# A decoder block on eight Trainium2 cores: a new order of loads and norms in its first stage, with unread matmuls on TensorE

## The reference, cut to what matters

```python
u = rms_norm(h, norm_mix[l])
proj = u @ w_in[l]                       # q | k | v (3 dilation groups x 8 heads x 64) | pool | gates
q = partial_rope(q, pos); k = partial_rope(k, pos)
att = dilated_attention(q, k, v)         # 3 groups: (window, dilation) = (128,1), (512,4), (2048,16)
...                                      # pooling mixer, gates, w_out, SwiGLU, final norm
```

## Time and profile before

| | us |
|---|---|
| median of 3 runs (lowest, highest) | 1216.14 (1214.82, 1222.4) |
| the profiled execution | 1215.8 |
| its span on the slowest core (core 5); all cores | 1214.3; 1207.6 to 1214.3 |
| TensorE busy in the span | 1155.9 (95%) |

### The profile page before, as it was taken

How to read it: one execution, slowest core, us unless ns; L and a number is a source line. 1 busy time by engine, 2 the same in 40 slices (tenths; PEclk the granted TensorE clock), 3 DMA queues, 4 the chain that set the end, 5 groups by cost and what they waited for, 6 DMA issues and landing times.

```text
span 1214.3 us, 21698 instructions; the slowest of 8 cores (1207.6 to 1214.3 us)
## 1 busy us (share of the span) xinstructions
PE 1155.9 (95%) x8470; PEld 644.7 (53%) x8470; DVE 575.4 (47%) x883; ACT 443.9 (37%) x728; POOL 68.9 (6%) x134
## 2 busy tenths in 40 slices
PE   3888899999999999799999999999999999999997
PEld 2454766586676666344444444444444444444477
DVE  3346566755654558875333467422213233122455
ACT  3464545745655564563222133311120032111213
POOL 0001000000001110100111100000000000000000
PEclk9899999999999999999999999999999999999999
DMA  8837633233323331212555523244612813446733
GB/s 201 235 113 207 138 80 75 48 76 80 76 50 81 76 58 40 53 22 39 136 146 111 76 46 52 53 74 88 115 28 52 148 35 70 78 80 112 154 116 106
DMA packets 33764, 109.98 MB, mean 91 GB/s; under 512 B 4736, under 2 KB 12160, under 8 KB 27776
## 3 DMA queue, kind: packets, MB, share of 16 engines
q0 software_dynamic: 15264, 69.76, 30.8%
q1 hardware_dynamic: 18400, 38.84, 11.0%
HBM read 148.31 MB, written 16.06 MB: 135 GB/s over the span
## 4 chain that ended last, share of the span: by engine, by line
PE 87%; DVE 5%; DMA 3%; ACT 2%; issue 2%; SPq 0%; DVEq 0%; POOL 0%; ACTq 0%; POOLq 0%
PE ps_p L197 50%; PE ps_s L197 18%; PE ps_o L197 16%; PE ps_o L200 3%; DMA wp<-w_in 1%; DVE uto L210 1%; DMA rin<-qk 1%; DVE ta L207 1%; DVE rt L207 1%; ACT rs L204 1%; DMA qk<-rout 1%; DVE acc L207 1%; DMA rout<-rp 0%; DVE uth L210 0%; DVE ftv L210 0%
## 5 line engine op out<-in xcount | busy, mean ns | idle before, releaser
L197 PE MATMUL ps_p<-uto,wp 128*128 128x512 bf16 (+1 forms) x784 | 182.7, 386 | 15.7 <-DVE uto L210 6.9
L197 PE MATMUL ps_s<-ftv,wguv 128*128 128x512 bf16 x640 | 144.7, 379 | 0.0
L197 PE MATMUL ps_o<-ftv,wguv 128*128 128x512 bf16 x640 | 144.7, 379 | 0.0
L197 PEld LDWEIGHTS ps_p<-uto,wp 128*128 128x128 bf16 x784 | 76.2, 100 | 108.2 <-issue 27.9
L197 PE MATMUL ps_p<-actt,wdv 128*128 128x512 bf16 (+2 forms) x704 | 115.7, 326 | 0.0
L204 ACT ACTIVATE qk<-ps_p 128x512 bf16<-128x512 f32 (+2 forms) x122 | 69.8, 577 | 108.4 <-PE ps_p L197 95.0
L207 DVE TENSOR_TENSOR acc<-ps_o,acc 128x1024 f32<-128x1024 f32 x32 | 64.9, 2030 | 84.6 <-PE ps_s L197 51.1
L197 PEld LDWEIGHTS ps_s<-ftv,wguv 128*128 128x128 bf16 x640 | 62.6, 98 | 75.5
L197 PEld LDWEIGHTS ps_o<-ftv,wguv 128*128 128x128 bf16 x640 | 62.6, 98 | 75.6
L197 PEld LDWEIGHTS ps_p<-wp,uto 128*128 128x128 bf16 x1536 | 95.0, 122 | 6.5 <-issue 1.8
L197 PE MATMUL ps_p<-wp,uto 128*128 128x128 bf16 x1536 | 97.7, 225 | 0.8 <-ACT qk L204 0.8
(11 more groups left out here) (120 smaller groups left out, 1433.3 us busy)
## 6 DMA issues: line engine op xcount, KB each, us to landing
wguv<-wgu POOLq DMA_DIRECT2D x20, 1024.0 KB, 7.7
wp<-w_in POOLq DMA_DIRECT2D x12, 768.0 KB, 7.4
wdv<-wd POOLq DMA_DIRECT2D x6, 1408.0 KB, 19.3
ht<-x SPq DMA_DIRECT2D x32, 256.0 KB, 5.0
xs<-x SPq DMA_DIRECT2D x3, 2048.0 KB, 17.6
xs<-x POOLq DMA_DIRECT2D x3, 2048.0 KB, 10.4
xs<-x SPq DMA_DIRECT2D x4, 1024.0 KB, 17.7
oT<-ost SPq DMA_DIRECT2D x12, 256.0 KB, 2.9
```

The lines of the kernel that those rows point to most:

```text
L197: return P.op("pe", lambda e: e.matmul(out, lhsT=lhsT, rhs=rhs, start=start, stop=stop), after)
```

## The change

- Loads: the second half of piece 0 is issued only when the first has landed, and pieces 2 to 7 each when the piece before has landed. The weights of unit 1 wait for the second half of piece 0, where they waited for half of piece 1. The masks wait for piece 3. Pieces 6 and 7 change buffers. The weights of unit 3 wait for the gather of unit 1.
- Squares: both halves' squares are issued ahead of the first items; some of the squares of pieces 1 and 2 go from ScalarE to VectorE; those of pieces 6 and 7 are cut in two and lie between other items.
- Items: unit 1 on piece 0 comes ahead of unit 0 on piece 1. Unit 0's v copies on own tokens go to ScalarE after piece 0.
- Attention: the first unit's steps start 13 items after its gather, the others' 15 as before.
- Ahead of everything a Ln of one column on ScalarE and 80 matmuls of 128x128 (the matrix of 1/1024 times itself) into `ps_o`, which nobody reads; 26 more of them after the sums of each half.

```diff
     def load_piece(i):
         if i == 0:
-            return [P.dma("sp", piece0[h], tile_of(x, 2048 * h, 8, 256), d_xh[0][h]) for h in range(2)]
+            t = P.dma("sp", piece0[0], tile_of(x, 0, 8, 256), d_xh[0][0])
+            return [t, P.dma("sp", piece0[1], tile_of(x, 2048, 8, 256), d_xh[0][1], after=[t])]
...
-        after = [t_u[(0, 1, 2, 4, 3)[i - 3]]] if i > 2 else [t_ld[1][1]]
+        after = [t_ld[i - 1][1]] + ([t_u[i - 3]] if i > 2 else [])
         if i == 7:
             after = after + [t_in0[0]]
...
+            ts.append(tt(o, p, p, ALU.mult, after=[t_ld[i][c // 4]]) if (i == 1 and c in (1, 3)) or (i == 2 and c % 2) else
+                      act(o, p, AF.Square, after=[t_ld[i][c // 4]]))
...
+    def idle_mm(n):
+
+        for _ in range(n):
+            mm(ps_o[:, 0:128], onev, onev, True, True, after=[t_one])
+
+    def half_piece(h, ts):
...
         t = act(r, r, AF.Exp, after=[bank_free[k]], scale=-0.5)
+        idle_mm(26)
         for c in range(8):
...
-            if u < 2:
+            if u < 2 and not on_act:
                 t_v[u] = bank_free[k] = P.op("dve", lambda e: e.tensor_copy(out=outv, in_=inv), [t, slot_free[g]])
...
-            ready[v] = n_item[0] + LAG
+            ready[v] = n_item[0] + (LAG if v else 13)
...
-    t_wp.append(P.dma("pool", wpv[1], tile_of(w_in, 3072, 8, 384), d_wp[1], after=[t_ld[1][0]]))
+    t_wp.append(P.dma("pool", wpv[1], tile_of(w_in, 3072, 8, 384), d_wp[1], after=[t_ld[0][1]]))
     t_ld += [load_piece(2)]
-    t_msk = P.dma("pool", mskv, msk, P.dsem())
...
-    half_piece(0)
+    act(rsv[1][:, 0:1], onev[:, 0:1], AF.Ln, after=[t_one])
+    idle_mm(80)
+    half_piece(0, half_squares(0))
+    ts = half_squares(1)
     for item in half_items(0):
         run(item)
-    half_piece(1)
+    half_piece(1, ts)
...
-    normalize(1, sq[1])
-    t_ld.append(load_piece(3))
-    for item in of(0, 1):
-        run(item)
-    sq.append(squares(2))
-    load_wp(2, [t_ld[2][1]])
-    for k, item in enumerate(of(1, 0) + of(1, 1)):
+    for k, item in enumerate(of(1, 0) + of(0, 1) + of(1, 1)):
         run(item)
         if k == 1:
+            normalize(1, sq[1])
+            t_ld.append(load_piece(3))
+            load_wp(2, [t_ld[2][1]])
+            t_msk = P.dma("pool", mskv, msk, P.dsem(), after=[t_ld[3][1]])
+        if k == 3:
+            sq.append(squares(2))
+        if k == 6:
             normalize(2, sq[2])
             t_ld.append(load_piece(4))
...
-        if k == 3 and i + 2 < 7:
+        if k == 3 and i < 4:
             sq.append(squares(i + 2))
-
+        if i == 4 and k in (3, 5):
+            sq6.extend(squares(6, 2 * k - 6, 2 * k - 2))
...
         if k == 4:
-            normalize(6, sq[6])
-            att_done[:] = [t_u[6]] * 4
-        if k == 3:
+            normalize(6, sq6)
+        if k == 5:
+            load_wp(3, [t_in0[1]])
             t_tab.append(load_tab(2, []))
-            load_wp(3)
             load_wp(4)
-        if k == 10:
-            sq.append(squares(7))
-        if k == 12:
-            normalize(7, sq[7])
+        if k in (6, 8):
+            sq7.extend(squares(7, 2 * k - 12, 2 * k - 8))
+        if k == 9:
+            normalize(7, sq7)
+            att_done[:] = [t_u[7]] * 4
```

More of the change, by code:

```diff
@@ L250, in _body @@
     t_u = [None] * len(PIECES)
-    t_in0 = [None]
+    t_in0 = []
     t_uc = [[None] * 8 for _ in PIECES]
-    piece = [xbuf[i].rearrange("p (c t) -> p c t", c=8) for i in (0, 1, 2, 0, 1, 2, 1, 0)]
+    piece = [xbuf[i].rearrange("p (c t) -> p c t", c=8) for i in (0, 1, 2, 0, 1, 2, 0, 1)]
     piece0 = [xbuf[0][:, 2048 * h:2048 * h + 2048].rearrange("p (c t) -> p c t", c=8) for h in range(2)]
@@ L271, in u_of, with squares, half_squares @@
         return uth[:, :, t0:t0 + n] if t0 < 2048 else uto[:, :, t0 - 2048:t0 - 2048 + n]
-    def squares(i):
+    def squares(i, c0=0, c1=8):
         ts = []
-        for c in range(8):
+        for c in range(c0, c1):
             o, p = u_of(i)[:, c, :], piece[i][:, c, :]
-            ts.append(act(o, p, AF.Square, after=[t_ld[i][c // 4]]))
+            ts.append(tt(o, p, p, ALU.mult, after=[t_ld[i][c // 4]]) if (i == 1 and c in (1, 3)) or (i == 2 and c % 2) else
+                      act(o, p, AF.Square, after=[t_ld[i][c // 4]]))
         return ts
-    def half_piece(h):
+    def half_squares(h):
         u = [uto[:, c, 256 * h:256 * h + 256] for c in range(8)]
-        ts = [tt(u[c], piece0[h][:, c, :], piece0[h][:, c, :], ALU.mult, after=[t_ld[0][h]]) if c % 2 else
-              act(u[c], piece0[h][:, c, :], AF.Square, after=[t_ld[0][h]]) for c in range(8)]
+        return [tt(u[c], piece0[h][:, c, :], piece0[h][:, c, :], ALU.mult, after=[t_ld[0][h]]) if c % 2 else
+                act(u[c], piece0[h][:, c, :], AF.Square, after=[t_ld[0][h]]) for c in range(8)]
+    def idle_mm(n):
+        for _ in range(n):
+            mm(ps_o[:, 0:128], onev, onev, True, True, after=[t_one])
+    def half_piece(h, ts):
+        u = [uto[:, c, 256 * h:256 * h + 256] for c in range(8)]
         k, ps = take_bank()
@@ L338, in qk_item, with v_item @@
         return emit
-    def v_item(u, batch, i_src=None):
+    def v_item(u, batch, i_src=None, on_act=False):
         g = u % 3
@@ L580, in run @@
             rope_turn(v, t_in)
-            t_in0[0] = t_in0[0] or t_in
-            ready[v] = n_item[0] + LAG
+            t_in0.append(t_in)
+            ready[v] = n_item[0] + (LAG if v else 13)
         if turns and turns[0][0] <= n_item[0]:
@@ L663, in behind @@
                 t_tab.append(load_tab(i - 2, [t_ld[i + 2][1]]))
-        if k == 3 and i + 2 < 7:
+        if k == 3 and i < 4:
             sq.append(squares(i + 2))
+        if i == 4 and k in (3, 5):
+            sq6.extend(squares(6, 2 * k - 6, 2 * k - 2))
+    sq6, sq7 = [], []
     for i in range(2, 5):
```

4 lines of the change are left out of this document (2 added, 2 removed).

## The result

The changed kernel takes 1208.43 us (median of 8 runs, beside 1215.82 of the kernel before in the same session), a ratio of 0.9932 (95% interval 0.9919 to 0.9944). Some executions of either kernel are slower, with a lower clock on the cores of one die (two of these 8, 1263.39 and 1355.37), and since the ratio leaves these out it is not the quotient of the two medians. The profiled execution took 1208.4 us, with a span of 1206.9 on its slowest core, core 1 (1197.7 to 1206.9 over the cores). Forecast were 1206, with a range of 1196 to 1214.

The account below looks back on a forecast made before the run. TensorE bounds the kernel, with 35.2 us idle and some slow clock to win ahead of 160 us. Terms 3.8 + 0.78 + 1.85 + 1.91 + 1.27 = 9.6 off 1215.8 give 1206.2, forecast 1206, range 1196 to 1214.

Parts of the forecast that it names:

- piece 2's first sixteen end earlier: Start of the kernel: piece 2's first sixteen products end at 62.2 instead of 66.0, 3.8 us gained.
- v copies: Far unit's first bank: unit 0's copies on ScalarE, so VectorE's products no longer hold it, 0.78 us gained.
- squares of piece 6: Piece 6 lands at about 82, ahead of its squares, so TensorE's wait for a copy behind them goes, 1.85 us.
- first scores' wait: First attention scores waiting for unit 0's rotary: taken to stay at 2.4 us as now, 0 in the sum.
- masks: End of unit 0's attention: steps two items earlier remove the wait for a mask, 1.91 us gained.
- behind unit 3's start: The slow clock behind the mask wait goes, 24 matmuls in 5.34 instead of 6.61, 1.27 us gained.
- The price of the slow clock: Unit 1's sixteen matmuls on piece 0: clock falls at the wait for its weights, 3.3 us lost.
- what would make it wrong: Signs against the forecast: x pieces over 13 us each, sums waiting for squares, or clock down again behind piece 1 (3 us).
- for the reason given: Unread matmuls stand where TensorE waits anyway; any delay at half clock is covered by the wait for unit 1's weights.
- The step that failed: From 160 us on: time won earlier passes to the end, since TensorE's stream follows in the same order.
- the clean front: Rival at the start: clock stays up or unit 1's weights land by 26.6, rotary waited for 0.6; 1201 us, chance 0.30.
- The starved front: Slower rival: loads one behind another, pieces 2, 3 and 4 keep 17.6 us each; 1220 us, chance 0.05.

Follow-up runs that it names:

- e3: Changed kernel with x loads as eager as before: both halves at once, pieces 2 to 7 as soon as their buffer is free; 1209.38 us.
- e7: Changed kernel with unit 0's items on piece 1 ahead of unit 1's on piece 0, the order of before; 1205.04 us.
- e1: Changed kernel without its 132 unread matmuls; 1208.33 us.
- e5: Changed kernel with 36 more unread matmuls ahead of unit 1's first products and five behind each of seven paced matmuls on pieces 1, 2 and 4; 1205.27 us.
- e11: Changed kernel with the old item order, later units' first scores one item later, and unread matmuls ahead of piece 1's products and within pieces 1 and 4; 1203.09 us.
- e2: Changed kernel with the first unit's attention steps 15 items after its gather, as before the change, instead of 13; 1209.26 us.
- e8: Changed kernel with the squares of pieces 6 and 7 in one group each instead of two; 1209.17 us.
- e6: Changed kernel with the first scores of every unit but the first one item later; 1206.30 us.
- e4: Changed kernel with 36 more unread matmuls ahead of unit 1's first products, where TensorE waits for the weights; 1207.16 us.

## Why the prediction was right, and where its sum was not

The time fell where it was forecast, by the mechanism forecast, up to unit 3: 9.5 us on the profiled cores (9.8 by medians). Behind unit 3 a step failed. Term by term, from the rows of both profiled executions; three rows of the kernel before that the table needs and that stand nowhere above (a v copy, piece 4's products at full speed, piece 7's sums):

```profile
75.54 0.61 PE L197 MATMUL ps_p<-uth,wp 128*128 128x128 bf16 x8 [0.78 <-DVE v L356]
...
85.82 2.10 PE L197 MATMUL ps_p<-uto,wp 128*128 128x512 bf16 x9 [0.29 <-DVE uto L210]
...
130.42 1.89 PE L197 MATMUL ps_p<-uth,one_s 128*128 128x512 bf16 x8 [1.29 <-ACT v L204]
```

| term | forecast | measured |
|---|---|---|
| piece 2's first sixteen end earlier (66.0 to 62.8) | 3.8 | 3.2 |
| v copies | 0.78 | 0.5: both waits of 0.78 gone, one of 1.03 for a qk copy in their place |
| squares of piece 6 | 1.85 | 1.85, by its landing and not by the split |
| copies behind piece 7's squares | 0 | 1.29 |
| first scores' wait | 0 | 0.57 |
| masks | 1.91 | 1.86 |
| other rows up to unit 3 | 0 | 0.2 |
| behind unit 3's start | 1.27 | -2.1 |
| sum | 9.6 | 7.4 |

The 0.2 of the other rows is a balance: the slow clock behind piece 4 costs 1.6 (3.71 for nine instead of 2.10) and piece 7's sums 0.9 (2.78 instead of 1.89), and smaller rows give 2.7. Up to unit 3 the terms that were forecast come to 7.4 instead of 8.3, and 2.1 that was not forecast (1.29, 0.57 and 0.2) lifts this to 9.5; behind unit 3 the forecast misses by 3.4 the other way. That the total lies as near to the forecast as it does is in part luck. Two figures of the prediction don't follow as written, 24.1 and 1.9 to 26.6 (26.0) and the third load at 82 (81); neither enters the sum.

- **The start.** Second half landed 18.6 (17 forecast), unit 1's first product 30.3 (29.8), piece 2's sixteen 62.8 (62.2). The price of the slow clock was over-sized at its place, 1.7 instead of 3.3 on core 1 and nothing on five cores, and fell a second time behind piece 1 for 1.5, which the text had named as what would make it wrong; that the two together are what was written for one is luck. e3 shows the loads as the part that brings the start forward. The new order of items, which the forecast took as it stood and gave no price of its own, costs 2.4 at unit 3 (e7).
- **The unread matmuls** cost nothing and give nothing in the time, as forecast, and for the reason given (e1). The rule cited from the Trainium skill (TensorE: Matmul & The Clock Gate, What's actually happening), that activity releases the throttle, fits the rows in part: behind 106 unread matmuls the first v item is at 1.06 on four cores, without them on none, but on the other four it stays at 1.25 to 1.91. They stand in the wrong place for a gain: e5 and e11 put them into the paced stretches.
- **The masks** are the forecast's 1.91, which e2 brings back.
- **Piece 7.** "at most 1 us either way" for the wait for piece 7's squares was too small: the kernel before waits 1.29 on the slowest core, 2.5 to 2.8 on five others, for a v copy queued behind them, and e8 gives 1.5 for the split.
- **The step that failed** is "a microsecond won there passes to the end, since what follows is a stream on TensorE in the same order". The stream has first scores in it that wait for a transfer. In the kernel before, the last shuffle of one unit (`rout`) was issued at 264.81 and its scores ran at 276.33, 11.5 us later; now it is issued at 257.38 and the scores are due at 266.4, 9.0 later, since unit 0's two items less pull all later steps forward. The way back takes `qk<-rout` 4.2 to 4.5 us on four cores, which wait for nothing, and 5.4 to 6.0 on the other four, which wait, the slowest core among them. With an item more (e6) the waits are gone. The slow row itself is gone too (24 products take 5.35 at 147.42 instead of 6.61), but its 1.27 does not reach the end: cores without rotary waits take 1059.4 to 1059.5, whereas the two cores of the kernel before that had no slow row there (6 and 7) took 1058.8 and 1058.5. The rest on core 1, 1061.9, is 3.4 longer than core 5's before without its slow row: 2.3 for the rotary waits, 0.4 for more waits for qk copies (1.2 instead of 0.8), and 0.7 whose cause stays open.

The last shuffle and the first scores behind it, in the kernel before and then in the changed one (266.4 is 267.44 less the wait of 1.03):

```profile
264.81 0.59 POOL L96 DMA_DIRECT2D rout<-rp  x1 [33.58 <-DVE rp L207]
...
276.33 0.40 PE L197 MATMUL ps_s<-qk 64*128 64x128 bf16 x8
```

```profile
257.38 0.59 POOL L96 DMA_DIRECT2D rout<-rp  x1 [35.47 <-DVE rp L207]
...
267.44 0.40 PE L197 MATMUL ps_s<-qk 64*128 64x128 bf16 x8 [1.03 <-DMA qk<-rout]
```

Of the rivals, the clean front had its mechanism half right: with the clock held up (e5) unit 3 starts 3.2 earlier, but the change as it stands doesn't hold it. The rival spoke of one wait, e5 fills three stretches besides, and e4, which fills that wait alone, gains nothing; so that 3.2 is near the 3.3 it was given is chance. The starved front did not come: pieces 2 to 7 took 8.8 to 13.1 us each.

## What to carry to other kernels

Between the last gap that an edit removes and the end there may be a transfer that was only just covered: follow each later wait's slack before a microsecond is passed on, on the core that will be slowest. A stretch of matmuls that another engine paces costs its own waits and can cost a slow clock behind it (here behind piece 1's on every core, behind the later ones on some or none). Matmuls that nobody reads helped when they stood inside the stretches (e5) and not when they stood ahead of them alone (e4). An order that lets the pace and the slow clock fall on the same matmuls pays only once, as I read e7. Where the queues are full, try one load at a time in the order of need (3.3 us at unit 3 in e3).

## What the runs showed of the hardware

- The granted clock reads 1.00 from the start of the span until its first recorded fall, although the 128x128 matmuls of a v item in that time take 119 ns each on e1's core 7, and 66 behind 106 unread ones on core 1 of the changed kernel: ahead of its first event the column didn't tell the two speeds apart.
- One transfer of the same size at the same place, `qk<-rout` of unit 1, issued at 254 to 261 us, takes 4.2 to 4.5 us on four cores and 5.4 to 6.0 on the others.
- With unread matmuls in one wait alone the clock fell behind piece 1's paced stretch on all cores and behind piece 2's on six (e4); with five unread matmuls behind each paced one as well it read 1.00 from 28 to 160 us on seven cores (e5).
